# Attention in an encoder layer: who splits the probabilities into high and low halves, and how a query tile's maxima are moved

## The reference

```
s = einsum("bqgrd,bkgd->bgrqk", q_blk, k) * HEAD_DIM ** -0.5
p = softmax(s, axis=-1)
o = einsum("bgrqk,bkgd->bqgrd", p, v)
```

## Time and profile before

| | us |
|---|---|
| median of 3 runs | 2684.73 (2683.97 to 2686.51) |
| profiled execution | 2687.89 |
| its span, first to last instruction | 2686.1 |
| PE busy | 2582.1 (96%), 11174 matmuls |
| DVE busy | 1718.4 (64%) |
| POOL busy | 1530.5 (57%) |
| ACT busy | 947.7 (35%) |
| mean granted TensorE clock | 0.986 of full |

### The profile page before, as it was taken

How to read it: one execution, slowest core, us unless ns; L and a number is a source line. 1 busy time by engine, 2 the same in 40 slices (tenths; PEclk the granted TensorE clock), 3 DMA queues, 4 the chain that set the end, 5 groups by cost and what they waited for, 6 DMA issues and landing times.

```text
span 2686.1 us, 38512 instructions
## 1 busy us (share of the span) xinstructions
PE 2582.1 (96%) x11174; PEld 2064.3 (77%) x11174; DVE 1718.4 (64%) x1839; ACT 947.7 (35%) x1345; POOL 1530.5 (57%) x1023
## 2 busy tenths in 40 slices
PE   7999999999599999997999999999999999999999
PEld 5778787887466777765888888888888878888887
DVE  6996399999499999985566434356733535673351
ACT  5443111212154545444343323334322323442231
POOL 3335777676378999994445444444544444444444
PEclk9999999999799999998999999999999999999999
DMA  4333222322732111115422234542222454232233
GB/s 160 115 117 130 84 71 73 91 65 82 148 75 58 48 40 47 47 30 173 142 95 96 94 99 137 173 149 95 100 94 95 132 168 156 98 102 94 96 100 117
DMA packets 152621, 274.35 MB, mean 102 GB/s; under 512 B 53456, under 2 KB 66384, under 8 KB 152400
## 3 DMA queue, kind: packets, MB, share of 16 engines
q1 hardware_dynamic: 152528, 273.20, 32.3%
HBM read 222.16 MB, written 48.76 MB: 101 GB/s over the span
## 4 chain that ended last, share of the span: by engine, by line
PE 52%; DMA 1%; POOL 0%; DVE 0%; ACT 0%; issue 0%; SPq 0%; POOLq 0%; DVEq 0%; ACTq 0%
PE t_ps L62 17%; PE t_ps L64 17%; PE t_ps L63 17%; DMA t_wraw<-w_tail_t 1%; POOL t_wlo L1755 0%; DMA t_x<-mix_scratch 0%; DVE t_hlo L1865 0%; ACT t_whi L1769 0%; DVE t_x L1929 0%; PE t_ps L1963 0%; SPq L1728 0%; ACT t_hhi L1775 0%; SPq L1661 0%; SPq L1688 0%; SPq L1671 0%
## 5 line engine op out<-in xcount | busy, mean ns | idle before, releaser
L1755 POOL TENSOR_TENSOR t_wlo<-t_wraw,t_whi 128x1024 fp32r<-128x1024 f32 x266 | 670.7, 2522 | 794.6 <-ACT t_whi L1769 794.6
L1769 ACT ACTIVATE t_whi<-t_wraw 128x1024 fp32r<-128x1024 f32 x266 | 281.6, 1059 | 619.5 <-PE t_ps L64 552.3
L1371 POOL TENSOR_TENSOR a_plo<-a_p,a_phi 128x512 fp32r<-128x512 f32 x320 | 452.6, 1440 | 60.6 <-DVE a_phi L1459 60.6
L62 PE MATMUL t_ps<-t_hhi,t_whi 128*128 128x512 f32 x960 | 374.7, 390 | 0.0
L62 PE MATMUL t_ps<-t_ahi,t_whi 128*128 128x512 f32 x960 | 373.6, 389 | 0.4 <-POOL t_wlo L1755 0.4
L64 PE MATMUL t_ps<-t_hhi,t_wlo 128*128 128x512 f32 x960 | 373.5, 389 | 0.0
L63 PE MATMUL t_ps<-t_alo,t_whi 128*128 128x512 f32 x960 | 373.5, 389 | 0.0
L64 PE MATMUL t_ps<-t_ahi,t_wlo 128*128 128x512 f32 x960 | 373.5, 389 | 0.0
L63 PE MATMUL t_ps<-t_hlo,t_whi 128*128 128x512 f32 x960 | 373.4, 389 | 0.0
L1929 DVE TENSOR_TENSOR t_x<-t_ps,t_x 128x512 f32 (+1 forms) x96 | 66.4, 692 | 373.6 <-PE t_ps L64 373.6
L1459 DVE CAST a_phi<-a_p 128x512 fp32r<-128x512 f32 x320 | 258.7, 816 | 44.1 <-ACT a_p L1402 42.5
(11 more groups left out here) (231 smaller groups left out, 4784.7 us busy)
## 6 DMA issues: line engine op xcount, KB each, us to landing
t_wraw<-w_tail_t SPq DMA_DIRECT2D x266, 512.0 KB, 3.3
a_q<-roped_scratch SPq DMA_DIRECT2D x144, 128.0 KB, 2.7
w_raw<-w_in_t SPq DMA_DIRECT2D x32, 512.0 KB, 4.1
proj_scratch<-s_gate SPq DMA_DIRECT2D x48, 256.0 KB, 2.1
t_graw<-proj_scratch SPq DMA_DIRECT2D x24, 512.0 KB, 4.6
roped_scratch<-p_r_hi SPq DMA_DIRECT2D x30, 256.0 KB, 2.0
roped_scratch<-p_r_lo SPq DMA_DIRECT2D x30, 256.0 KB, 2.3
t_graw<-mix_scratch SPq DMA_DIRECT2D x14, 512.0 KB, 4.4
```

The lines of the kernel that those rows point to most:

```text
L62: pe.matmul(out, whi, xhi, start=start, stop=False)
L1371: pool.tensor_tensor(p_lo[s][:], p32[s][:], f32(p_hi[s][:]), ALU.subtract).then_inc(plo_done, 1)
L1755: pool.tensor_tensor(w_lo[s][:], w_raw[s][:], f32(w_hi[s][:]), ALU.subtract).then_inc(wlo_ready, 1)
L1769: act.activation(w_hi[s][:], w_raw[s][:], ACT.Copy).then_inc(whi_ready, 1)
```

## The change

`p_hi` of the even steps is still cast by DVE, that of the odd steps is made by a copy on ACT, right behind the step's exponential. `p_lo` of the places 0, 2 and 3 is still subtracted by POOL, whose loop now has three subtractions; that of place 1 is subtracted by DVE, ahead of its cast for place 2. The two semaphores `phi_done` and `plo_done` become four, one for each maker, and those that wait ask the one that belongs to the place (`wait_plo`, with `four` as the number of the group of four steps).

The maxima of a unit are moved by one transfer. For that the queries are dealt to the tiles in another way: tile j holds the queries 4 p + j, so a partition's four maxima are neighbours in the row. The weights of the maxima's matmul are then every fourth column of `q1`.

In the gates' stage, POOL does one `alone` before the copy of `rotations`, 8 times in all.

```diff
--- before.py
+++ after.py
@@ -978,6 +978,7 @@
                         link(pool.tensor_tensor(c, low_im, t_re, ALU.mult))
                         link(pool.tensor_tensor(top_im, top_im, c, ALU.add))
                     if part == 2:
+                        alone(pool, st.turn)
                         link(pool.tensor_copy(rot[b.par][:, :, :, 0:CH_A], rot[b.par][:, :, :, CH_A:2 * CH_A]))
                         pool.sem_inc(rot_ready, 1)
 
@@ -1232,8 +1233,10 @@
         max_found = sem("a_max_found")
         scored = sem("a_scored")
         exp_done = sem("a_exp_done")
-        phi_done = sem("a_phi_done")
-        plo_done = sem("a_plo_done")
+
+
+        phi_dve, phi_act = sem("a_phi_dve"), sem("a_phi_act")
+        plo_dve, plo_pool = sem("a_plo_dve"), sem("a_plo_pool")
         pv_done = sem("a_pv_done")
         ln_done = sem("a_ln_done")
         rden_done = sem("a_rden_done")
@@ -1265,6 +1268,17 @@
                 return None
             return 1 + d
 
+        def four(sq, it, kv, kt):
+
+            return it * sq.n + (sq.s0 + kv * sq.n + kt) // QKP
+
+        def wait_plo(eng, quad, s, back):
+
+            if s == 1:
+                eng.wait_ge(plo_dve, quad + (1 if back else 2))
+            else:
+                eng.wait_ge(plo_pool, 3 * quad + ((0, None, 1, 2)[s] + (1 if back else 4)))
+
         def left_over(sq, off):
 
             return range(off // sq.n, -1, -1)
@@ -1294,10 +1308,9 @@
 
                     u = sq.u0 + it * 4 + kv
                     s = kv
-                    for j in range(BLK // P):
-                        sp.wait_ge(max_found, 4 * u + (3 + j))
-                        sp.dma_start(f32(q2[s][HEAD:HEAD + 1, j * P:(j + 1) * P]),
-                                     f32(nmax[s][:, j:j + 1])).then_inc(nmax_in[s], 16)
+                    sp.wait_ge(max_found, 4 * u + (2 + BLK // P))
+                    sp.dma_start(f32(q2[s][HEAD:HEAD + 1]).rearrange("o (p j) -> o p j", p=P),
+                                 f32(nmax[s][:])).then_inc(nmax_in[s], 16)
 
                 def store(u, kv, head, blk):
 
@@ -1363,13 +1376,13 @@
                                                    (k2[HEAD:HEAD + 1], 1.0))):
                     pool.memset(f32(part), value).then_inc(ones_set, 1)
                     pool.wait_ge(ones_set, n + 1)
-                pool.sem_inc(plo_done, QKP)
+                pool.sem_inc(plo_pool, 3)
                 with pool.Fori(0, STEPS // QKP) as i:
-                    for s in range(QKP):
-                        pool.wait_ge(phi_done, QKP * i + (s + 1))
+                    for s, phi_done, n in ((0, phi_dve, 1), (2, phi_dve, 2), (3, phi_act, 2)):
+                        pool.wait_ge(phi_done, 2 * i + n)
                         pool.wait_ge(pv_done, QKP * i + (s + 1))
                         pool.tensor_tensor(p_lo[s][:], p32[s][:], f32(p_hi[s][:]),
-                                           ALU.subtract).then_inc(plo_done, 1)
+                                           ALU.subtract).then_inc(plo_pool, 1)
 
             @block.scalar
             def _(act):
@@ -1398,9 +1411,14 @@
                             for kt in range(sq.n):
                                 step = it * (4 * sq.n) + (sq.s0 + kv * sq.n + kt)
                                 act.wait_ge(scored, step + 1)
-                                act.wait_ge(plo_done, step + 1)
+                                wait_plo(act, four(sq, it, kv, kt), kt % QKP, True)
                                 act.activation(p32[kt % QKP][:], ps[:, ST_BANK + kt % 2], ACT.Exp,
                                                scale=HEAD ** -0.5).then_inc(exp_done, 1)
+                                if kt % 2:
+                                    act.wait_ge(exp_done, step + 3)
+                                    act.wait_ge(pv_done, step + 1)
+                                    act.activation(p_hi[kt % QKP][:], p32[kt % QKP][:],
+                                                   ACT.Copy).then_inc(phi_act, 1)
                                 d = due(sq, LN_STEP, it, kv, kt)
                                 if d:
                                     act.wait_ge(pv_done, step + (1 + QKP - LAG))
@@ -1420,6 +1438,7 @@
             def _(dve):
                 dve.sem_inc(max_found, 2)
                 dve.sem_inc(normed, 2)
+                dve.sem_inc(plo_dve, 1)
                 def find_max(sq, u, s, j):
 
                     dve.wait_ge(max_mm, 4 * u + (j + 1))
@@ -1454,9 +1473,15 @@
                         for kv in range(NKV):
                             for kt in range(sq.n):
                                 step = it * (4 * sq.n) + (sq.s0 + kv * sq.n + kt)
-                                dve.wait_ge(exp_done, step + 3)
-                                dve.wait_ge(pv_done, step + 1)
-                                dve.tensor_copy(p_hi[kt % QKP][:], p32[kt % QKP][:]).then_inc(phi_done, 1)
+                                if kt % QKP == 2:
+                                    dve.wait_ge(phi_act, 2 * four(sq, it, kv, kt) + 1)
+                                    dve.wait_ge(pv_done, step)
+                                    dve.tensor_tensor(p_lo[1][:], p32[1][:], f32(p_hi[1][:]),
+                                                      ALU.subtract).then_inc(plo_dve, 1)
+                                if kt % 2 == 0:
+                                    dve.wait_ge(exp_done, step + 3)
+                                    dve.wait_ge(pv_done, step + 1)
+                                    dve.tensor_copy(p_hi[kt % QKP][:], p32[kt % QKP][:]).then_inc(phi_dve, 1)
                                 d = due(sq, SCALE_STEP, it, kv, kt)
                                 if d:
                                     scale_out(it * 4 + (sq.u0 + kv - d), (kv + d) % 2)
@@ -1480,14 +1505,14 @@
                         pe.wait_ge(max_found, 4 * u + (j + 1))
                     bank = MX_BANK + (j if sq is A else 2 * (j % 2) + half)
                     key0 = (sq.kt0 + 4 * half) * P
-                    mm = pe.matmul(ps[:, bank], q1[s][:, j * P:(j + 1) * P],
+                    mm = pe.matmul(ps[:, bank], q1[s][:].rearrange("d (p j) -> d j p", p=P)[:, j],
                                    k1[:, s, key0:key0 + BLK], start=True, stop=True)
                     if half == per - 1:
                         mm.then_inc(max_mm, 1)
 
-                def output(sq, unit, s, kt, step):
-
-                    pe.wait_ge(plo_done, step + 1 + QKP)
+                def output(sq, unit, s, kt, step, quad):
+
+                    wait_plo(pe, quad, kt % QKP, False)
                     if kt == 0:
                         pe.wait_ge(normed, unit + 1)
                     out, tile = ps[:, O_BANK + s % 2], sq.kt0 + kt
@@ -1524,7 +1549,7 @@
                             ahead, s_ahead = unit + 2, (kv + 2) % 4
                             sq_ahead = next_seq(sq, last, kv)
                             n_of = lambda k: it + (sq.u0 // 4 + 1 + (1 if k >= NKV else 0))
-                            pe.wait_ge(nmax_in[kv], n_of(kv) * 64)
+                            pe.wait_ge(nmax_in[kv], n_of(kv) * 16)
                             pe.wait_ge(q_in[kv], n_of(kv) * 48)
                             if sq_ahead is not sq and sq_ahead:
                                 pe.wait_ge(k_first_in[1], 32)
@@ -1543,12 +1568,14 @@
                                     for part in range(sq_ahead.n // sq.n):
                                         max_part(sq_ahead, ahead, s_ahead, kt * (sq_ahead.n // sq.n) + part)
                                 if kt >= LAG:
-                                    output(sq, unit, kv, kt - LAG, step - LAG)
+                                    output(sq, unit, kv, kt - LAG, step - LAG, four(sq, it, kv, kt - LAG))
                                 elif not (isinstance(it, int) and it == 0 and kv == 0):
-                                    output(sq, unit - 1, (kv + 3) % 4, kt - LAG + sq.n, step - LAG)
+                                    output(sq, unit - 1, (kv + 3) % 4, kt - LAG + sq.n, step - LAG,
+                                           four(sq, it, kv, kt - LAG))
                     for_iterations(pe, sq, iteration)
                     for kt in range(sq.n - LAG, sq.n):
-                        output(sq, sq.u0 + 4 * sq.iters - 1, 3, kt, sq.s0 + (4 * sq.iters - 1) * sq.n + kt)
+                        output(sq, sq.u0 + 4 * sq.iters - 1, 3, kt, sq.s0 + (4 * sq.iters - 1) * sq.n + kt,
+                               four(sq, sq.iters - 1, 3, kt))
 
 
 TAIL_T = 2 * KD + KD + 2 * (D_FF // P)
```

## The result

| | before | after |
|---|---|---|
| median of 4 runs each, us | 2684.89 (2683.97 to 2686.51) | 2641.59 (2640.54 to 2643.30) |
| profiled execution, us | 2687.89 | 2643.30 |
| its span, us | 2686.1 | 2641.5 |
| DVE / POOL / ACT busy, us | 1718.4 / 1530.5 / 947.7 | 1629.9 / 1388.0 / 1043.8 |

The ratio of the times is 0.9836, with an interval of [0.9824, 0.9849]: 43.3 us faster.

What follows compares the result with a forecast made beforehand. The DVE-POOL lock was taken to set the attention's pace, with TensorE as floor: 11.1 (A) + 19.5 (B) + 3.3 (last steps) = 33.9, less 3 kept back, 31 us off; 2654 us on the runs' footing, range 2645 to 2676.

Steps and rivals of the forecast that it cites:

- One transfer of maxima: Attention, SyncE's queue: one transfer per unit replaces four; nothing gained in B, tight in A, gains before the 5.5 us stall lost.
- The kept 3 us: Held back from the summed gain of 33.9 us for waits the walk of steps doesn't see; ends 0 and 7.
- B: Attention steps of sequence B, 241 counted: from 1.484 to TensorE's floor of 1.403 us a step, 19.5 us gained.
- A: Attention steps of sequence A, 53 counted: from 1.66 to 1.45 us a step, 11.1 us gained.
- The last steps: Attention's last 14 steps, where no maxima are left: from 1.457 to 1.22 us a step, 3.3 us gained.
- The lock: Attention: DVE and POOL shut each other out, setting the old pace; DVE's new subtraction taken at 1.2 us, range 0.7 to 1.7.
- ACT's copies: Attention, odd steps: ACT copies of 0.633 us hidden behind TensorE; cost taken as nothing, 24 us at most.
- Strided weights: The maxima's 320 weight loads, taking every fourth query: cost taken as nothing, at most 0.09 us a step, 29 us.
- Rival 1: Maxima's weight loads: the strided load shows on TensorE, 14 to 29 us back, 2668 to 2682; chance 0.20.
- Rival 2: Attention: DVE becomes the bound and slower, its subtraction and casts held in full by POOL, about 2703 us; chance 0.06.
- Rival 3: A gains nothing because queries wait on SyncE behind the last maximum: 11 us less, 2665; chance 0.10.
- Rival 4: Attention: the DVE-POOL port never handed on without a gap; A unchanged, B at 1.45 us a step, 2673; chance 0.06.

Runs made afterwards that it cites:

- One transfer alone: Kernel before the change, given only the single transfer of a unit's maxima and its every-fourth-query weights; casts and subtractions as before: 2680.47 us, ratio 0.9979.
- the deal alone: Changed kernel (casts and subtractions shared among DVE, ACT, POOL) with the four maxima transfers and contiguous weights put back, against the kernel before: 2652.49 us, ratio 0.9872.

## Why the prediction was wrong, point by point

**The step that failed** is "One transfer of maxima", in its last sentence: "steps gained before it are lost in it, and they are left out". It gave steps 0 to 12 nothing, and they gave 8.0 us. One transfer alone gave 7.2 us there; the deal alone gave 17.91 - 16.50 = 1.4 and 8.32 - 7.51 = 0.8, so for the deal the sentence was nearly right. I took the stall's end as fixed by B's keys. It is fixed by all that stands in the queues ahead of the queries, and the part that the change removes, a thousand four-byte packets ahead of the keys and five hundred behind them, was the slow one: in the kernel before, packets that started from 717 to 720 us moved 35 GB/s, and in the changed kernel 208. I had priced the three issues that leave SyncE's queue and not their packets. A price for them stood nowhere in my argument; the DMA rate around 718 us would have shown it.

**The kept 3 us** were not needed. Without them and with the 8.0, the sum would have been 41.9, off the profiled execution 2646, on the runs' footing 2642.8.

**B** was under-sized by 3.6 us, in two parts. Its steps were 1.491 us before by their starts, and I had 1.484 from the line's first and last start: 236 x 0.007 = 1.7. And the floor was 1.393, not 1.403: 236 x 0.010 = 2.4 (the forecast counted 241 steps, which takes 0.4 off again). Most of the second is the 0.007 us that a step with strided weights is shorter than one with contiguous ones. Seven profiles with a stride are at 1.393, and the only kernel without that reaches TensorE's pace is at 1.400; why is open.

**A** at 1.45 us a step was right: 1.449. But of the 0.056 above B's pace only part is the waits that I had given as the reason. Four of these 48 steps have a seventh matmul, 292 matmuls in all, and at 0.232 us each they need 67.8 us, 1.41 a step; the other 1.7 us are waits. The seventh matmul I had not worked out, and the guess covered it.

**The last steps**, 3.3 us, were right at 3.2.

**The lock** as the cause of the old pace was right. The kernel without DVE's subtraction has fewer instructions on DVE and is slower, with POOL busy or kept from starting by a cast for 323.7 of 325 us. The Trainium skill's rule (SBUF — State Buffer, "SBUF: two separate sides") agrees with the 0.95 us of a subtraction on DVE that starts while POOL's runs. The size that I gave it was off: in a gap of POOL's it was to be had at 0.67 us, and the order of the steps lets 14 of A's 16 and 29 of B's 64 fall there. I had 1.2 from a row where at least half of the records are held, although my own walk of the steps had the subtraction on a free port, from 3.7 to 4.35.

**ACT's copies** cost nothing, as I had it (B is at TensorE's pace with them), and are worth more than the subtraction: without them A is at 1.821 and the time 2669.45, without the subtraction it is 2657.59.

**Strided weights** at nothing was right, though the row I took it from was not this load: it is 0.12 us longer, and hidden. The Trainium skill's rule (SBUF — State Buffer, "Door 1: The DMA port swizzle"), that going to a new line of 16 bytes each time has a price, agrees with the load's 0.31 against 0.19 us. TensorE's 0.232 us a matmul doesn't show it.

**Rivals.** Rival 1 fell (with strided loads B is at 1.491 as before, or at 1.393). Rival 2 is real without ACT's copies only, in A, at 1.821. Rival 3 is real with four issues behind the last maximum, at 1.661; with the one issue of the change A doesn't show it. Rival 4 fell: TensorE waits 7.0 us for POOL.

**Signs.** The attention ended near 1177 and not 1190; of the 14 us, 8 are the first twelve steps, 4 are B and 3 the reserve, and A gives 1 back. I had written that a gain over 40 us would mean a misread floor or lock. It meant neither: the misread was a queue.

## What to carry to other kernels

Before a stall on a transfer is written down as fixed, list everything that stands ahead of that transfer in its queues, by packets and not by bytes, and look at the DMA rate in short slices there: 6 KB in four-byte packets, 4 KB ahead of the keys and 2 KB behind them, held the queries up here by some 5 us, the time of a megabyte at the 208 GB/s of the same stretch. And read a DMA share with the slice before it, since a packet that stands is counted where it starts. When two engines share a lock, don't price an instruction by a row in which they collide; walk the order of the steps and see whether it falls in the other's gap. And when a change joins two edits that look unrelated, build the sum for each alone, as the runs here did: the large one came out as forecast, if in part by luck, and the small one was where the larger error lay.

## What the runs showed of the hardware

- Eight transfers within SBUF of 128 four-byte packets each, into one partition, were followed by 16 packets of 4 KB that lasted 2.3 to 3.2 us each, where others took 0.32, and the packets that started in a stretch of 3 us moved 35 GB/s; behind eight transfers of 32 packets of 16 bytes, with the same bytes in all, it was 216 GB/s and no packet lasted over 1.5 us.
- A 128x128 weight load that takes every fourth float of a row took 0.309 us on average against 0.19 for neighbouring floats, and cost nothing between matmuls of 512 columns that start 0.23 us apart.
- A stall of 5.5 us on TensorE was followed by a granted clock of 0.50 in the next stretch of 5 us, one of 1.66 us by 1.00; in the kernel before that was worth 1.7 us on top of the stall.
- A subtraction on DVE with two sources in SBUF took 0.67 us where POOL was idle, 0.95 where it started 0.4 us before POOL's ended, and up to 1.59 in the last steps of B; the same kind took 1.78 at the median in the projection.
